# Moving the rounding and splitting of single weight chunks within the ScalarE and VectorE queues of a two-block transformer kernel

## What is computed

```python
f_in, f_gate, g_u, g_v, g_gate, c_q, c_kv, k_rope, a_gate = _split_in(h @ w_in)
f_out = (_fourier(f_in) @ w_fmix) * silu(f_gate)
g_out = _spatial_gate(g_u, g_v, g_ln_g, g_ws, g_bs) * silu(g_gate)
q = rmsnorm_heads(rmsnorm(c_q, q_a_g) @ w_uq)        # 8 heads of 96
k, v = split(rmsnorm(c_kv, kv_a_g) @ w_ukv)          # k with k_rope, normed per head
o = attend(rope(q), rope(k), v) * silu(a_gate)
x = x + gate * (concat(f_out, g_out, o) @ w_out)
```

## Time and profile before

| | before |
|---|---|
| time of the runs, us | 917.99 median of 3 (916.62 to 918.2) |
| time of the profiled execution, us | 916.97 |
| its span, us | 915.2 |
| mean granted TensorE clock | 0.981 |
| PE, DVE, ACT busy, us | 870.4, 640.2, 447.6 |
| DMA moved | 138.02 MB |

### The profile page before, as it was taken

How to read it: one execution, slowest core, us unless ns; L and a number is a source line. 1 busy time by engine, 2 the same in 40 slices (tenths; PEclk the granted TensorE clock), 3 DMA queues, 4 the chain that set the end, 5 groups by cost and what they waited for, 6 DMA issues and landing times.

```text
span 915.2 us, 13495 instructions
## 1 busy us (share of the span) xinstructions
PE 870.4 (95%) x5412; PEld 721.6 (79%) x5412; DVE 640.2 (70%) x1267; ACT 447.6 (49%) x759; POOL 21.2 (2%) x16
## 2 busy tenths in 40 slices
PE   8999799979999985999999999999999999999996
PEld 5678377856678774887998888898999988888885
DVE  5444837576637749776679999987778766655666
ACT  3352415535524436365544444465655565555552
POOL 0000000000000000000001121100000000000000
PEclk9999989989999998999999999999999999999998
DMA  9785443120245131422365656442265366556551
GB/s 356 270 304 190 184 157 107 38 70 1 92 162 182 54 115 31 143 69 92 105 198 184 188 180 201 167 156 76 70 202 193 120 204 201 175 196 202 174 177 47
DMA packets 40719, 138.02 MB, mean 151 GB/s; under 512 B 4432, under 2 KB 4560, under 8 KB 40400
## 3 DMA queue, kind: packets, MB, share of 16 engines
q1 hardware_dynamic: 40224, 134.41, 43.6%
q10 hardware_dynamic: 432, 2.74, 0.8%
HBM read 136.08 MB, written 1.05 MB: 150 GB/s over the span
## 4 chain that ended last, share of the span: by engine, by line
PE 68%; DVE 25%; ACT 3%; DMA 2%; issue 1%; SPq 0%; DVEq 0%; ACTq 0%
PE ps L415 8%; DVE wlo L1484 7%; PE ps L985 6%; DVE AF L1963 6%; PE ps L370 4%; PE ps L371 4%; PE ps L416 4%; PE ps L375 4%; PE ps L747 3%; PE ps L489 2%; PE ps L398 2%; PE ps L770 2%; PE ps L387 2%; PE ps L399 2%; DMA AF<-wmod 2%; PE ps L402 2%
## 5 line engine op out<-in xcount | busy, mean ns | idle before, releaser
L1484 DVE TENSOR_TENSOR wlo<-raw,whi 128x1024 fp32r<-128x1024 f32 (+3 forms) x213 | 240.6, 1154 | 31.6 <-ACT whi L1023 31.4
L1023 ACT ACTIVATE whi<-raw 128x1024 fp32r<-128x1024 f32 (+3 forms) x213 | 211.3, 1001 | 101.5 <-DMA raw<-wpack 54.7
L370 PE MATMUL ps<-hx,whi 128*128 128x256 f32 (+1 forms) x384 | 116.8, 304 | 15.9 <-DVE wlo L1484 15.6
L415 PE MATMUL ps<-hx,whi 128*128 128x512 f32 x320 | 113.9, 398 | 0.0
L371 PE MATMUL ps<-hx,whi 128*128 128x256 f32 (+1 forms) x384 | 113.8, 296 | 0.0
L375 PE MATMUL ps<-hx,wlo 128*128 128x256 f32 (+1 forms) x332 | 98.6, 297 | 0.0
L370 PEld LDWEIGHTS ps<-hx,whi 128*128 128x128 f32 x384 | 74.9, 195 | 20.9 <-DVE wlo L1484 17.2
L416 PE MATMUL ps<-hx,wlo 128*128 128x256 f32 x320 | 89.8, 281 | 0.0
L371 PEld LDWEIGHTS ps<-hx,whi 128*128 128x128 f32 x384 | 74.9, 195 | 1.8 <-issue 0.2
L460 PE MATMUL ps<-whi,hx 128*128 128x512 f32 (+1 forms) x192 | 71.5, 372 | 3.3 <-DVE lat L1618 3.3
L415 PEld LDWEIGHTS ps<-hx,whi 128*128 128x128 f32 x320 | 60.1, 188 | 14.6
(11 more groups left out here) (301 smaller groups left out, 1685.1 us busy)
## 6 DMA issues: line engine op xcount, KB each, us to landing
raw<-wpack SPq DMA_DIRECT2D x181, 512.0 KB, 4.2
AF<-wmod SPq DMA_DIRECT2D x48, 512.0 KB, 6.4
raw<-wpack SPq DMA_DIRECT2D x24, 256.0 KB, 2.8
raw<-wpack SPq DMA_DIRECT2D x6, 384.0 KB, 3.2
XT<-xin SPq DMA_DIRECT2D x4, 512.0 KB, 5.8
raw<-wpack SPq DMA_DIRECT2D x4, 432.0 KB, 4.8
cst<-cpack ACTq DMA_DIRECT2D x1, 1093.0 KB, 8.0
AF<-l2rows ACTq DMA_DIRECT2D x1, 1024.0 KB, 7.3
```

Source lines behind the costliest of these rows:

```text
L370: e.matmul(o, wh[:, b], xh(k), start=j == 0, stop=False, skip_group_check=True)
L415: e.matmul(ps.ap(key, 512).rearrange("p (s n) -> p s n", s=2), wh[:, b], K.hx[:, :, k, 0:256], start=k == 0, stop=False, skip_group_check= ...
L1023: e.activation(W.hi(i), W.raw(i), ACT.Copy).then_inc(*HI.up(j))
L1484: e.tensor_tensor(W.lo(i), W.raw(i), W.hi(i), ALU.subtract).then_inc(*LO.up(j))
```

## The change

Neither PE's nor SP's queue changes, and no instruction's work. On ACT and DVE:

- Layer 0: the rounding of fgate(1) stands in front of gvkr's takes, its subtraction behind the latents' norms. `w12()` (which rounds the two chunks after it and copies W12) stands in front of the squares of q.
- Layer 0, attention step 8: ACT rounds ggate(1) in front of q's takes (the call names uq(1,0), and `highs` goes four chunks beyond it), DVE subtracts gu(0) in front of the gate of agate(3) (`lows` goes three beyond).
- Layer 1: the roundings of gvkr's second and third weight and of ukv stand behind the latents' copies and squares, both fin and the mod row, not between them; on DVE the rests stand in front of the subtractions of gvkr's second and third weight. The rests wait for ACT's squares, and the PSUM banks are given on by DVE's event alone (this in both layers).
- Layer 1: fgate(0) is rounded in front of gvkr's takes and subtracted behind the latents' norms; fgate(1) is rounded in front of the heads' squares and subtracted behind g_v's norm.

```diff
--- before.py
+++ after.py
@@ -1107,14 +1107,16 @@
 
         def fin(m):
             key = (l, "fin", m)
-            highs(wkey(*key), NHL - 1 if l else 2)
+            highs(wkey(*key), 1 if l else 2)
             ac.wait_ge(M[key], *bar)
             e.activation(g.fi[:, m, cs], ps.ap(key, N), ACT.Copy).then_inc(*A.up(key))
             ps.give(key, A.now())
 
         for m in range(2):
-            highs(wkey(l, "cq", m), NHL - 1 if l else 2)
-        highs(wkey(l, "ckv", 0), NHL - 1 if l else 2)
+            highs(wkey(l, "cq", m), 0 if l else 2)
+        highs(wkey(l, "ckv", 0), 0 if l else 2)
+        if l:
+            highs((l, "fin", 1), 1)
         for m in range(2):
             key = (l, "cq", m)
             ac.wait_ge(M[key], K.c1["cst"], *bar)
@@ -1131,6 +1133,7 @@
         for i in range(3):
             highs((l, "gvkr", "w", i), 1)
         highs((l, "uq", l, 1), 0)
+        highs((l, "fgate", 1 - l), 0)
         ac.wait_ge(M[l, "gvkr"])
         if l == 1:
             e.activation(K.rs[0:32, 0:256], ps.ap((l, "kf"), 256, parts=slice(0, 32)), ACT.Copy).then_inc(*A.up((l, "kf")))
@@ -1190,8 +1193,8 @@
         if l == 0:
             squares("k", 0, 0, 0, V[l, "krb", 0])
             q_take(0, 1, M[l, "cqsum"])
+            w12()
             squares("q", 0, 1, 1)
-            w12()
             mod_row(3)
             silu("fgate", 1, g.fg[:, 1, :])
             mod_row(4)
@@ -1204,6 +1207,7 @@
             kn_take(1, 0, M[l, "kT", 0, 1, 4])
         else:
             kn_take(1, 2)
+            highs((l, "fgate", 1), 0)
             squares("k", 0, 0, 0, V[l, "krb", 0])
             squares("k", 1, 2, 2, V[l, "krb", 1], V[l, "gvr"])
             q_take(1, 1, M[l, "cqsum"], M[l, "kfT"])
@@ -1271,6 +1275,7 @@
             if l == 0 and i == 7:
                 heads_T("k", 1, 0, 1)
             if l == 0 and i == 8:
+                highs((l, "uq", 1, 0))
                 q_take(1, 0, M[l, "kT", 1, 1, 4])
             if l == 0 and i == 9:
                 squares("q", 1, 0, 2, V[l, "rope", "k", 1])
@@ -1606,17 +1611,19 @@
             lows((l, nm, m))
 
         for nm, m in FIRST if l == 0 else FIRST[:5]:
-            lows(wkey(l, nm, m), NHL - 2 if l else 2)
+            lows(wkey(l, nm, m), 0 if l else 2)
+        if l:
+            lows((l, "fin", 1), 1)
         dv.wait_ge(K.c1["cst"], *bar)
         for m in range(2):
             key = (l, "cq", m)
-            dv.wait_ge(A[key])
+            dv.wait_ge(A[l, "cqsq", m])
             e.scalar_tensor_tensor(out=g.cql[:, m, :], in0=ps.ap(key, N), scalar=C("qag", 2 * l + m, 1), in1=g.cqh[:, m, :], op0=ALU.mult, op1=ALU.subtract).then_inc(*V.up((l, "cql", m)))
-            ps.give(key, A[l, "cqsq", m], V.now())
+            ps.give(key, V.now())
         key = (l, "ckv", 0)
-        dv.wait_ge(A[l, "ckv"])
+        dv.wait_ge(A[l, "ckvsq"])
         e.scalar_tensor_tensor(out=K.ckvl, in0=ps.ap(key), scalar=C("kvag", l, 1), in1=K.ckvh, op0=ALU.mult, op1=ALU.subtract).then_inc(*V.up((l, "ckvl")))
-        ps.give(key, A[l, "ckvsq"], V.now())
+        ps.give(key, V.now())
         for i in range(3):
             lows((l, "gvkr", "w", i), 1)
         tab = []
@@ -1643,6 +1650,7 @@
         ps.give((l, "st"), V.now())
         rsqrt(g.stat[:, t0:8], g.stat[:, 120 + t0:128], g.stat[:, 128 + t0:136])
         V.mark((l, "stat"))
+        lows((l, "fgate", 1 - l), 0)
         if l:
             bias(1, 5)
 
@@ -1798,6 +1806,7 @@
         else:
             kv_take(1, 2)
             gv_norm()
+            lows((l, "fgate", 1), 0)
             hsum("k", 0, 0, 0, 0)
             hsum("k", 1, 2, 2, 2)
             hsum("q", 1, 1, 1, 1)
@@ -1889,6 +1898,8 @@
                     heads_T("k", 1, 0, 0)
                 if i == 7:
                     heads_T("k", 1, 0, 1)
+                if i == 8:
+                    lows((l, "uq", 1, 0))
                 if i == 9:
                     hsum("q", 1, 0, 2, 2)
                 if i == 10:
```

## The result

The changed kernel took 893.31 us, the median of four runs (892.88 to 897.61), against 918.1 us before (916.62 to 919.18). The ratio is 0.9742 with a 95% interval of 0.9709 to 0.9774, so 24.8 us faster. The forecast was 891.3 us with a range of 886 to 901.

The account below looks back on a forecast made before the run. The prediction took PE as the bound, busy 870.4 of 915.2 us. Its terms, 10.9 + 5.1 + 4.4 + 5.3 = 25.7, came off the profiled 916.97 us: 891.3 us, range 886 to 901.

Parts of the forecast that it names:

- Layer 0, fgate(1): Layer 0's fourier part: PE's waits of 1.68 and 6.08 us go and 3.1 us of clock return; gain 10.9 us.
- Layer 0, attention: Layer 0's attention: an earlier DMA shortens PE's 5.47 us wait for ACT's copy of p; gain 5.1 us, bounds 3.3 and 6.9.
- 1.8 of clock returns: Term in layer 0's attention: 1.8 us lost to PE's lower clock comes back when the wait for p shrinks.
- Rival 1: PE pays half clock behind four or five short waits; 6.6 us of clock not won, 897.9 us; chance 0.13.
- Layer 1, latents: Layer 1's latents: PE's 3.31 us wait for the last rest shrinks and clock returns; gain 4.4 us, bounds 2.0 and 5.0.
- Layer 1, fgate: Layer 1's fgate(0) and (1): PE's 9.51 us wait for four subtractions goes; gain 5.3 us, bounds 4.1 and 7.4.
- They wait for that: DVE becomes the bound: Layer 1: PE's transposes wait 1.8 us for DVE's end of g_u, so the gain is DVE's 5.3 us.
- a half clock after the 2.8 us wait before dft is hidden in these 1.8: Layer 1: lower clock behind the dft wait costs nothing extra, as PE waits 1.8 us for DVE at the transposes anyway.
- Rival 2: Layer 1's gate wins nothing, as DVE's chain reaches g_u hardly earlier; 5.3 us more, 896.6 us; chance 0.12.
- Rival 3: Roundings moved forward on ACT wait for their chunk's DMA, in both layers; about 920 us; chance 0.03.
- a sign of being wrong: Signs named: clock under 1.00 behind short waits, a DMA releasing a moved rounding, PE waiting for w1's low part (layer 1).
- the clock's price: Time PE lost at its lower clock behind the waits in both layers, 8.3 us; the sum was said to be smaller by that.

Follow-up runs that it names:

- kernel five: The changed kernel with only DVE's layer 0 subtraction for fgate(1) put back behind the head norms and vf copies; early rounding and W12 copies stay: 903.58 us.
- kernel one: The changed kernel with layer 0's fourier part taken back (fgate(1)'s rounding and subtraction, W12's copies): 903.28 us.
- ten: The changed kernel with the further edits of kernels seven, eight and nine together: 887.92 us.
- two: The changed kernel with layer 0's attention step 8 taken back (ggate(1)'s early rounding and gu(0)'s early subtraction removed): 897.86 us.
- four: The changed kernel with layer 1's fgate(0) and fgate(1) rounded and subtracted where they were before: 897.77 us.
- three: The changed kernel with the order at layer 1's latents taken back, the PSUM banks again given on by two events: 898.25 us.
- six: The changed kernel with W12's copies behind the squares of q again: 891.86 us.
- eight: The changed kernel with layer 1's vf copies on DVE put in front of the two subtractions: 890.49 us.
- nine: Kernel eight with agate(1)'s subtraction also moved behind the heads' copies: 889.67 us.
- eleven: The changed kernel itself, unedited, measured and profiled a second time: 891.98 us.
- kernel seven: The changed kernel with gu(0)'s and ggate(1)'s subtractions both behind agate(3)'s gate in layer 0's attention step 8: 890.18 us.

## Why the prediction was right, and where not

*Layer 0, fgate(1): right.* 10.9 said, 11.14 found. Both waits went, the gaps took the rounding and the subtraction, the clock stayed at 1.00, and dft did not wait. That the late subtraction is the cause, and that the early rounding and W12 win nothing without it, kernel five shows. The rule in this step, that without idle time in front there is no half clock, held here but not 20 us earlier, as the last section shows. One thing my sum treated as separate is not: the W12 wait of 1.68 us had no price of its own before, since PE would have waited for DVE by that much longer (8.01).

*Layer 0, attention: mechanism right, size off.* Said 5.1, found 3.6 in the first profile and 4.6 where the clock held. The term that was wrong is "1.8 of clock returns": the new wait for p, 1.42 us as forecast (1.4), brought the lower clock back in some executions (0.83 in 180 to 190 us). With the clock held, PE's new waits were 0.48 us for agate(3)'s gate and 1.42 for p, together 1.9 where I had set 1.8; of the 0.5 us still missing then, the runs place no more than that 0.1. Rival 1 (the clock stays low) held at this place, in this profile, and the time moved by 1.0 us, not by its 1.8.

*Layer 1, latents: right.* 4.4 said, 2.83 + 1.51 = 4.34 found, with 0.47 us of wait left for the last rest (0.4 said) and no wait for w1.

*Layer 1, fgate: 5.3 said, 6.1 found, and the reason was wrong: a hit by luck.* PE's wait before the dft came out as worked out (2.81, said 2.8). The failing step is "They wait for that: DVE becomes the bound". I had put PE's transposes at 387.07 and DVE's end of g_u at 386.80 side by side and taken the nearness for a wait. It is the third group, 2.6 us later, that needs g_u. So "a half clock after the 2.8 us wait before dft is hidden in these 1.8" failed as well: PE took 13.88 instead of 12.08 us from the dft to the transposes, 1.8 on the path. The two errors went opposite ways: 2.1 us (7.4 won at the dft, by the working, less the 5.3) for a wait that PE did not have, and 1.8 for the clock. The rest of the 0.8 is the dft itself, which started 7.9 us earlier and not 7.4. With the clock held, as in kernel one, the step is worth 7.4 us (32.28 against 39.65 from W12 to the first scores), and PE's wait for DVE is 0.4 us, not 1.8. Rival 2 (nothing won here) fell.

*Rival 3* (a moved rounding waits for its chunk) fell in layer 0: the early rounding ran at 80.24, when PE was done with gvkr's second weight, not when its DMA landed. In layer 1 fgate(0)'s rounding did wait for its DMA (2.27 us, up to 321.42), but ended 1.9 us before gvkr's takes could start. So a DMA did release a moved rounding, which the prediction had named as a sign of being wrong, as it had a clock under 1.00 behind short waits (0.83 and 0.90 here). Both signs came; the first cost nothing, the second 1.0 and 1.8 us.

*The sum.* 11.14 + 3.59 + 4.34 + 6.13 = 25.2 against 25.7. In the first profile 1.52 us were lost between the first sums and ukv of layer 0, a place with no term in the prediction. That is why it took 892.88 and not about 891.3; in the second profile, where this place was undisturbed, the kernel took 890.99. One sum in the prediction is off: without the clock's price it would be 6.6 us smaller, not 8.3, because the 1.8 behind layer 1's gate never stood in it.

## What to carry to other kernels

Where one engine runs late once per stage, list the gaps of the helper engines before that point: a piece of work that is ready early and stands last in an in-order queue (here a 1.2 us subtraction behind 20 us of norms) can cost eight times its length (9.9 us here), and putting it into a gap cost nothing. Before calling an engine the new bound, read which instruction really waits for it, and not which one starts next to it in time. And price a stall of TensorE with the lower clock that may follow it: 1.3 to 3 us behind those of 3.3 to 9.5 us here, and anything from nothing to 3 us behind those of 1.4 to 2.8, where nothing in the stage had been changed.

## What the runs showed of the hardware

**The clock can fall without any idle time in the records.** In layer 0 TensorE runs 24 products with a single moving column (the sums over latents, rows L610 and L614). In the changed kernel's first profile there is no idle time around them, and the clock falls to half of its full rate within a microsecond of their end:

```profile
79.98 1.84 PE L610 MATMUL ps<-cst,wk 128*128 128x1 f32 x16
81.68 1.03 PE L614 MATMUL ps<-cst,acc 128*128 128x1 f32 x8
82.57 0.38 PE L460 MATMUL ps<-whi,hx 128*128 128x288 f32 x1
...
83.61 0.44 PE L460 MATMUL ps<-whi,hx 128*128 128x288 f32 x1
```

Products of 288 columns then take 0.24 us from start to start, instead of 0.13, up to 86.5. The kernel before, at the same place:

```profile
84.00:86.00 2.00, 2.00 (x17) 1.98 (x15) 0.51 (x4) 0.00 (x0) 0.00 (x0) 1.00 0.00 0
```

It is a matter of the execution: PE's queue is the same up to there in all kernels here; of thirteen profiles (before, the changed kernel twice, kernels one to ten) the stage took 10.24 or 10.25 us in three (the changed kernel's first, kernels one and two) and 8.72 or 8.73 in the ten others. That these sums bring the fall is not shown: layer 1 runs 16 such products, and no profile has a fall behind them.

The same holds behind the wait of 1.42 us in the attention: 1.0 us more in the changed kernel's first profile and in kernels four and five, nothing in kernels one, three, six, eight, nine and eleven. There is a third such place, behind the wait of 2.81 us before layer 1's dft. Eight profiles have that wait, and from the dft to the first scores they took 18.01 us (kernel one, clock 1.00), 19.03 to 19.28 (six of them) and 20.51 (kernel seven). The first two places make 1.5 and 1.0 us between two executions of the same program, the third up to 2.5 between kernels whose layer 1 is the same. That is as large as several of the edits here. Up to the first sums, where PE's work is the same in all kernels, the profiles took 79.98 to 81.99 us as well. For edits of that size the stages between landmarks tell more than the medians, and a stage with a wait in it is still only as good as the clock behind the wait.

The Trainium skill (TensorE: Matmul & The Clock Gate, "The HAM clock gate") describes the gate as watching how busy the engine has lately been, and says of the slow stretch at a kernel's start that its length is run-variable. These profiles show the same of falls in mid-kernel, with 8.72 or 10.25 us for the same stage. Its section "HAM oscillation — how this bites in real kernels" names idle gaps as what brings the fall; the one above came with no idle gap in the records, behind 24 products of one column each.
